# Rotary embedding of queries and keys: half-head rotation by four shifted copies on ScalarE in place of a TensorE product

## What is computed

```python
def apply_rope(t, cos, sin):
    half = t.shape[-1] // 2
    tf = t.astype(jnp.float32)
    t1, t2 = tf[..., :half], tf[..., half:]
    return jnp.concatenate([t1 * cos - t2 * sin, t2 * cos + t1 * sin], axis=-1).astype(t.dtype)
```

## Time and profile before

| | |
|---|---|
| median of 3 runs | 1289.53 us (1288.16 to 1290.08) |
| the profiled execution: its own time | 1289.31 us |
| the profiled execution: its span | 1287.7 us |
| PE busy | 1255.5 us, 98% of the span |
| DVE busy | 652.0 us, 51% |
| ACT busy | 270.4 us, 21% |
| granted TensorE clock, mean | 0.999 of full speed |

### The profile page before, as it was taken

The page is one execution under the profiler, slowest core; times in us unless marked ns, Lnnn a source line. Parts: engine busy times, 40 slices in busy tenths (PEclk is TensorE's granted clock), DMA queues, the critical chain, the costliest instruction groups (busy, mean ns, idle before and its releaser), DMA issues.

```text
span 1287.7 us, 26831 instructions
## 1 busy us (share of the span) xinstructions
PE 1255.5 (98%) x10748; PEld 953.2 (74%) x10748; DVE 652.0 (51%) x1636; ACT 270.4 (21%) x713; POOL 75.2 (6%) x134
## 2 busy tenths in 40 slices
PE   6999999999999999999999999999999999999997
PEld 4768888999999768689999997777764455445444
DVE  5355564888888533656677675664541011101104
ACT  4332304211111512630000013146300000000001
POOL 0100000000000000000000000100010000000020
PEclk9999999999999999999999999999999999999999
DMA  9999883577776672046776784894599999999990
GB/s 354 413 400 405 304 294 131 205 262 272 284 253 244 246 279 89 33 142 230 281 274 255 276 307 163 305 353 122 194 390 405 420 408 410 409 421 407 407 374 37
DMA packets 74181, 368.83 MB, mean 286 GB/s; under 512 B 8355, under 2 KB 8611, under 8 KB 49338
## 3 DMA queue, kind: packets, MB, share of 16 engines
q1 hardware_dynamic: 56594, 271.28, 55.5%
q0 software_dynamic: 17520, 96.64, 19.8%
HBM read 347.82 MB, written 20.06 MB: 286 GB/s over the span
## 4 chain that ended last, share of the span: by engine, by line
PE 94%; DVE 2%; ACT 2%; DMA 1%; SPq 1%; issue 0%; DVEq 0%
PE banks L972 20%; PE banks L704 18%; PE banks L1309 13%; PE banks L959 11%; PE banks L1358 9%; PE banks L1333 5%; PE banks L729 4%; PE banks L823 2%; PE banks L783 2%; PE banks L1039 2%; PE banks L888 1%; PE banks L872 1%; DMA ring<-stream 1%; PE banks L899 1%; PE banks L857 1%; PE banks L742 1%
## 5 line engine op out<-in xcount | busy, mean ns | idle before, releaser
L1750 DVE CUSTOM_DVE_ANT_0 side<-side 128x1024 f32<-128x1024 f32 x128 | 151.1, 1220 | 33.0 <-DMA side<-ada 32.9
L1309 PE MATMUL banks<-ring,arena 128*32 128x512 f32 x1536 | 166.3, 593 | 0.7 <-DVE arena L2232 0.7
L959 PE MATMUL banks<-arena,ring 128*128 128x256 f32 x704 | 160.2, 381 | 0.0
L704 PE MATMUL banks<-h,ring 128*128 128x256 f32 x640 | 143.5, 382 | 0.6 <-ACT arena L1408 0.3
L959 PEld LDWEIGHTS banks<-arena,ring 128*128 128x128 f32 x704 | 130.6, 191 | 16.8 <-issue 1.4
L704 PEld LDWEIGHTS banks<-h,ring 128*128 128x128 f32 x640 | 120.5, 190 | 21.7 <-issue 3.2
L1309 PEld LDWEIGHTS banks<-ring,arena 128*32 128x32 f32 x1536 | 50.1, 110 | 111.8 <-issue 110.8
L2335 DVE TENSOR_TENSOR arena<-arena,banks 128x256 f32<-128x256 f32 (+1 forms) x48 | 15.2, 330 | 178.5 <-ACT arena L1685 178.5
L704 PE MATMUL banks<-arena,ring 128*128 128x256 f32 x384 | 84.1, 380 | 0.5 <-ACT arena L1499 0.5
L972 PEld LDWEIGHTS banks<-h,ring 128*128 128x128 f32 x672 | 81.5, 192 | 2.0
L972 PE MATMUL banks<-arena 128*128 128x128 f32 x672 | 81.9, 276 | 0.0
(11 more groups left out here) (337 smaller groups left out, 1556.5 us busy)
## 6 DMA issues: line engine op xcount, KB each, us to landing
ring<-stream SPq DMA_DIRECT2D x247, 512.0 KB, 5.6
ring<-experts SPq DMA_DIRECT2D x96, 1024.0 KB, 14.8
side<-ada POOLq DMA_DIRECT2D x64, 1024.0 KB, 7.7
side<-experts SPq DMA_DIRECT2D x24, 1024.0 KB, 14.7
arena<-experts SPq DMA_DIRECT2D x8, 1024.0 KB, 14.8
yrows<-side POOLq DMA_DIRECT2D x1, 6144.0 KB, 42.4
hrows<-side POOLq DMA_DIRECT2D x1, 5632.0 KB, 20.4
arena<-lasts SPq DMA_DIRECT2D x8, 512.0 KB, 14.5
```

The costliest lines, as they stand in the source:

```text
L704: last = pe.matmul(bank(u, a, a + T), ring[:, s, (k0 + kc) * P:(k0 + kc + 1) * P], moving[:, kc, :], start=(kc == 0), stop=(kc == kn - 1))
L959: last = pe.matmul(banks[:, 4 + c // 2, (c % 2) * T:(c % 2 + 1) * T], ring[:, s, c * P:(c + 1) * P], hid[:, j % 2, :], start=False, stop=F ...
L1309: ins = pe.matmul(banks[BLOCK * j:BLOCK * (j + 1), t, :], hg[:, k, BLOCK * t:BLOCK * (t + 1)], ring[:, m, (j % 2) * 512:(j % 2 + 1) * 512] ...
L1750: dve.tensor_tensor_reduce(weights, weights, cond[:, 0 if layer0 else 1, :], 1.0, 0.0, ALU.mult, ALU.add, accum_out=msum[:, n:n + 1]).then ...
```

## The change

PE no longer rotates: the matrix `rotate`, the 20 rotation units and their places in the order of banks are gone. ACT makes the rotated tile instead, in `turn`: four copies of 32 partitions by 256, each from the neighbouring block of 32 partitions, with scale 1 or -1, into one of three buffers `ropet` in SBUF. The source is the PSUM bank, just before the bank is read by the usual copy (`take_turned`), or for r = 5 and 6 the tile in SBUF. From r = 3 on, ACT first waits until rope r-3 is complete. DVE multiplies the rotated tile by sin in place, in SBUF. With the rotation units gone, two projection units in a row are on different banks, where before a unit, a rotation and the next unit put the two units on the same bank.

```diff
-            def rotate(r, moving, ready):
-                u = U["rot", r]
-                begin(u)
-                pe.wait_ge(*ready)
-                pe.matmul(bank(u, 0, T), mat("rotate"), moving, start=True, stop=True).then_inc(aux_done, 1)
-
...
             between = {0: [lambda: one(("sq", 0))],
-                       1: [lambda: one(("sq", 1)), rot_of(0, "sq", 0, sqT[:, 0])],
-                       2: [lambda: one(("sq", 2)), rot_of(1, "sq", 1, sqT[:, 1])],
...
+                       1: [lambda: one(("sq", 1))],
+                       2: [lambda: one(("sq", 2))],
...
+            def turn(r, source):
+
+                if r >= 3:
+                    act.wait_ge(s_rope, r - 2)
+                for j in range(4):
+                    to, at = BLOCK * j, BLOCK * (j ^ 1)
+                    act.activation(ropet[to:to + BLOCK, r % 3, :], source[at:at + BLOCK, :], ACT.Copy, scale=(1.0 if j % 2 else -1.0))\
+                       .then_inc(s_turn, 1)
+
+            def take_turned(r, u, out):
+
+                act.wait_ge(*u.done)
+                turn(r, bank(u, 0, T))
+                take(u, out, 0, T)
...
-            take(U["iq", 1], iqT[:, 1, :], 0, T)
+            act.wait_ge(s_raw, raw_step(4, 5))
+            turn(5, ikT)
+            turn(6, iqT[:, 0, :])
+            take_turned(7, U["iq", 1], iqT[:, 1, :])
             take(U["iwT"], iws.rearrange("p a n -> p (a n)"), 0, 16, scale=float(8 ** -0.5 * 64 ** -0.5))
             for c in range(2, 4):
-                take(U["iq", c], iqT[:, c, :], 0, T)
+                take_turned(6 + c, U["iq", c], iqT[:, c, :])
             for c in range(2):
-                take(U["dk", c], dkT[:, c, :], 0, T)
+                take_turned(10 + c, U["dk", c], dkT[:, c, :])
...
-            attend(odd_heads, {2 * (c - 4): [lambda c=c: take(U["dq", c], dqT[:, c, :], 0, T)] for c in range(4, 8)})
+            attend(odd_heads, {2 * (c - 4): [lambda c=c: take_turned(12 + c, U["dq", c], dqT[:, c, :])] for c in range(4, 8)})
...
             def rope(r, tile, source):
-                u = U["rot", r]
-                dve.wait_ge(*u.done)
-                dve.tensor_tensor(ropet[:, r % 2, :], bank(u, 0, T), sin[:, :], ALU.mult).then_inc(freed[u.bank], 1)
+                part = ropet[:, r % 3, :]
+                dve.wait_ge(s_turn, 4 * (r + 1))
+                dve.tensor_tensor(part, part, sin[:, :], ALU.mult).then_inc(s_rot, 1)
                 dve.wait_ge(*((s_raw, raw_step(4, 5)) if U[source].bank > 1 else taken(U[source])))
                 dve.tensor_tensor(tile, tile, cos[:, :], ALU.mult).then_inc(s_rot, 1)
-                dve.wait_ge(s_rot, r + 1)
-                dve.wait_ge(*taken(u))
-                dve.tensor_tensor(tile, tile, ropet[:, r % 2, :], ALU.add).then_inc(s_rope, 1)
+                dve.wait_ge(s_rot, 2 * r + 2)
+                dve.tensor_tensor(tile, tile, part, ALU.add).then_inc(s_rope, 1)
```

More of the change, by code:

```diff
@@ L72 @@
 MATS = {}
-for _name, _n in (("ident", 128), ("heads", 128), ("rotate", 128), ("causal", TRI), ("band", TRI),
+for _name, _n in (("ident", 128), ("heads", 128), ("causal", TRI), ("band", TRI),
                   ("upto", T), ("iota", CAP), ("small", 64)):
@@ L170, in plan_units @@
         add(("sq", c), 1)
-        add(("rot", c - 1))
     add(("sk", 0), 1)
-    add(("rot", 3))
     add("sv", 1)
-    add(("rot", 4))
     add_out("eo")
@@ L181, in plan_units @@
     add(("iq", 1), 1)
-    add(("rot", 5))
     add("iwT")
     add(("iq", 2), 1)
-    add(("rot", 6))
     add(("iq", 3), 1)
-    add(("rot", 7))
     add(("dk", 0), 1)
-    add(("rot", 8))
     add(("dk", 1), 1)
-    add(("rot", 9))
-    add(("rot", 10))
     add("dv", 2)
-    add(("rot", 11))
     add(("dq", 0), 1)
@@ L197, in plan_units @@
         add(("dq", c), 1)
-        add(("rot", 11 + c))
         if c == 4:
             add("rrow")
-    add(("rot", 19))
     add_out("oo")
@@ L326, in program @@
         cum = region(27, [T], 72)
-        ropet = region(29, [2, T])
+        ropet = region(29, [3, T])
         oT2 = region(32, [8, T])
@@ L386, in program @@
         s_forget, s_cum = sem("s_forget"), sem("s_cum")
-        s_rot, s_rope = sem("s_rot"), sem("s_rope")
+        s_rot, s_rope, s_turn = sem("s_rot"), sem("s_rope"), sem("s_turn")
         s_iscore, s_relu, s_isum, s_topk, s_dmask = (sem(n) for n in ("s_iscore", "s_relu", "s_isum", "s_topk", "s_dmask"))
@@ L1145, in sv_unit @@
                 token_unit(u, 1, 1, P, P, do_begin=False)
-            def rot_of(r, name, c, tile):
-                return lambda: rotate(r, tile, taken(U[name, c]))
             between = {0: [lambda: one(("sq", 0))],
-                       1: [lambda: one(("sq", 1)), rot_of(0, "sq", 0, sqT[:, 0])],
-                       2: [lambda: one(("sq", 2)), rot_of(1, "sq", 1, sqT[:, 1])],
-                       3: [lambda: one(("sq", 3)), rot_of(2, "sq", 2, sqT[:, 2])],
-                       4: [lambda: one(("sk", 0)), rot_of(3, "sq", 3, sqT[:, 3])],
-                       5: [sv_unit, rot_of(4, "sk", 0, skT)]}
+                       1: [lambda: one(("sq", 1))],
+                       2: [lambda: one(("sq", 2))],
+                       3: [lambda: one(("sq", 3))],
+                       4: [lambda: one(("sk", 0))],
+                       5: [sv_unit]}
             for k in range(5):
@@ L1165, in _ @@
             one(("iq", 1))
-            rotate(5, ikT, (s_raw, raw_step(4, 5)))
             few_per_token("iw")
             one(("iq", 2))
-            rotate(6, iqT[:, 0], (s_raw, raw_step(4, 5)))
             one(("iq", 3))
-            rotate(7, iqT[:, 1], taken(U["iq", 1]))
             one(("dk", 0))
-            rotate(8, iqT[:, 2], taken(U["iq", 2]))
             one(("dk", 1))
-            rotate(9, iqT[:, 3], taken(U["iq", 3]))
             def index_scores(m):
@@ L1190, in _ @@
             index_scores(1)
-            rotate(10, dkT[:, 0], taken(U["dk", 0]))
             u = U["dv"]
@@ L1196, in _ @@
                     index_scores(2 + n)
-            rotate(11, dkT[:, 1], taken(U["dk", 1]))
             one(("dq", 0))
@@ L1203, in step @@
                         one(("dq", c))
-                    rotate(11 + c, dqT[:, c - 1], taken(U["dq", c - 1]))
                 return step
@@ L1632, in _ @@
             take(U["fv", 1], fv[:, 1, :])
-            between = {c: [lambda c=c: take(U["sq", c], sqT[:, c, :], 0, T)] for c in range(4)}
-            between[4] = [lambda: take(U["sk", 0], skT, 0, T)]
+            between = {c: [lambda c=c: take_turned(c, U["sq", c], sqT[:, c, :])] for c in range(4)}
+            between[4] = [lambda: take_turned(4, U["sk", 0], skT)]
             between[5] = [lambda: take(U["sv"], sv.rearrange("p a n -> p (a n)"), 0, T)]
@@ L1654, in _ @@
             for c in range(4):
-                take(U["dq", c], dqT[:, c, :], 0, T)
-            attend(odd_heads, {2 * (c - 4): [lambda c=c: take(U["dq", c], dqT[:, c, :], 0, T)] for c in range(4, 8)})
+                take_turned(12 + c, U["dq", c], dqT[:, c, :])
+            attend(odd_heads, {2 * (c - 4): [lambda c=c: take_turned(12 + c, U["dq", c], dqT[:, c, :])] for c in range(4, 8)})
             squares(5)
@@ L2423, in _constants @@
     k, m = p, np.arange(P)[None, :]
-    put("rotate", (k == m - 32) * (m % HD >= 32) * 1.0 - (k == m + 32) * (m % HD < 32) * 1.0)
     dist = np.concatenate([p - np.arange(HALF)[None, :], HALF + p - t], 1)
```

## The result

The changed kernel takes 1291.56 us, the median of 14 runs (1288.95 to 1295.31), against 1289.08 (1288.16 to 1290.56, 14 runs) for the kernel before: a ratio of 1.0019, interval 1.0011 to 1.0028. I had forecast 1284.1 with a range up to 1289.4. The measured median lies outside the range, on the slower side; it is 2.5 us or 0.2% above the kernel before, which is also about what a measurement here can tell.

A forecast was written before the change was run, and what follows sets the result against it. PE, busy for 98% of the span, was taken as the bound. Over the 20 rotations, 4.9 + 1.6 + 1.0 + 0.7 - 0.65 - 2.3 = 5.2 us less gave 1289.31 - 5.2 = 1284.1 us, range 1280.5 to 1289.4.

The forecast's parts named there:

- the price of a turn: On ACT, four copies of 32 partitions at 0.28 us each, 1.12 us in front of the usual copy.
- second transpose behind the first: Attention steps of rotations 2, 16, 17, 18: PE's start goes from 1.59 to 2.17 us, 2.3 us more in all.
- iq2 behind the end of iq1: Rotation 5: iq1 and iq2 now share a bank, so iq2 waits for iq1's copy; 0.65 us more.
- index scores 2 behind the end of dk1: Rotations 9 and 10: start 2.2 us after dk1 instead of 2.88, so 0.7 us less.
- dq5 behind the end of dq4: Rotation 15: shared bank, start 1.76 us after dq4's end against 1.81 before; no change.
- the rival of the dear copies: Turns at 0.40 us a copy: seven places hanging on ACT pay 0.48 more each, 3.4 together, 1287.5 us; chance 0.13.
- the granted clock is 1.00 in both windows: PE stays at the 2.4 GHz level, busy throughout; the change leaves the clock as it is.
- The banks alternate: Rotations 1, 3, 6, 7, 8, 12, 13 between projection units: 3.5 us a unit instead of 4.19, 4.9 us less.
- ACT's wait for rope r-3 and the choice of keys: Rope wait put at nothing, a few tenths in the range; DVE's key choice at nothing, 1.3 us in the range.
- the rival "given back in the experts": Weights' DMA sets the pace in the experts, so arriving 5 us earlier helps nothing: 1289.3 us; chance 0.08.
- the hidden case: ACT's share is hidden, turns being cheap: each rotation gives back 0.6, 12 us less, 1277 us; chance 0.07.
- The four attention steps would pay: Rotations 2, 16, 17, 18: PE waits about 1.2 us for L1484 where it was 0.67; 4 x 0.58 = 2.3 us more.

The follow-up runs named there:

- The kernel whose waits are filled: Changed kernel plus 16 unused 128x256 products on PE ahead of iq2, dq5 and second transposes, where PE waits for ACT; 1287.21 us, ratio 0.9978.
- the last kernel: Copies turned in SBUF behind the usual copy, but turns 0, 1, 2, 4 directly behind their copies and turn 19 a step later; 1280.59 us, ratio 0.9918.
- the one-block kernel: Changed kernel with all four copies reading and writing partitions 0 to 31, rotation left out; 1283.08 us, ratio 0.9942.
- the profile without the shift: Changed kernel with each of the four copies reading the block it writes, so halves don't change places; 1291.46 us, one run.
- The kernel with alternating banks alone: Kernel before, products kept on PE, rotations 5 to 14 moved to banks 4 and 6 so successive units alternate banks; 1286.60 us, ratio 0.9978.
- the two kernels that split the condition: Changed kernel, rotation left out: one writes partitions 0 to 31 and reads four blocks (1293.71 us), the other the reverse (1292.45 us).
- the one with the usual copy first: Changed kernel with the usual copy freeing the bank first and the turn reading the SBUF tile behind it, later in attention steps; 1287.40 us, ratio 0.9978.

## Why the prediction was wrong

**The step that failed first is the price of a turn.** "I take 0.28, since these are also Copy from PSUM to SBUF without a pointer." The copies of the earlier trace rows all begin at partition 0, and they overlap. The new copies begin at partitions 0, 32, 64 and 96 in turn, and don't: 0.40. The run with everything in one block shows both at once, 0.27 and 1283.1 us. So at that price the rest of the sum was right, or 2 us too cautious. Why the step failed: I compared operation, shape and memory, and not where in the partitions the instruction before had begun; "the shift of partitions is unseen" stood among the rival's reasons only.

The Trainium skill, page "VectorE: DVE Perf Modes", section "Two Vector instructions with no wait between them", states a rule of this kind for VectorE: an instruction is held until all earlier ones have finished if its input or output starts in another quadrant of 32 partitions than the last one's there. The section is about VectorE; the kernels with 1.57, 1.17, 1.58 and 1.56 us behave as if ScalarE had the same rule.
The Trainium skill's page "ScalarE: Activation LUTs", section "What ACT_TABLE_LOAD costs", has 399 ns for such a copy and an overlap of 93 for copies in a row. An estimate from it with the overlap left out is 0.40 a copy and 1.60 a turn, as measured; with it, as I had set it beside the rows, the estimate is 306 ns, and the measured spacing of overlapping copies is 0.27.

**The places were right, their sizes not.** Where I said that PE hangs on ACT, each place came out some half a microsecond longer, and 4 x 0.12 = 0.48 is the difference in a turn:

- second transpose behind the first, in step 1 of the third layer: 1.59 before, 2.17 forecast, 856.86 - 854.15 = 2.71 measured;
- iq2 behind the end of iq1: 1.75 forecast, 798.97 - 796.58 = 2.39. Of the 0.64 more, 0.16 are turns 5 and 6: at 0.44 a copy they fill ACT from 793.43 to 796.91, past iq1's end, and turn 7 starts 796.94 - 796.58 = 0.36 behind it and not 0.2;
- index scores 2 behind the end of dk1: 2.2 forecast, 817.16 - 814.55 = 2.61;
- dq5 behind the end of dq4: 1.76 forecast, 850.59 - 848.34 = 2.25. I had put this place at no cost.

That is the rival of the dear copies, 7 x 0.48 = 3.4 us, 1287.5. I gave it 0.13. The kernel whose waits are filled, in which this loss stands almost alone, took 1287.2. So the dear copies alone, as I had priced them, leave a gain; they don't turn the sign.

**The second failure is a sentence and not a number**: "the granted clock is 1.00 in both windows [...]; the change leaves it so." I added to PE's waits for ACT in the plan and priced them at their length. Behind them the granted clock fell to the 1.2 GHz level in the profiles. In the changed kernel's first one, from 501.69 on, sixteen records and a unit took 9.0 us (501.69 to 510.7), where the kernel with copies in one block needed 507.37 - 501.64 = 5.7: a wait of 2.22 us cost 3.3 more behind it. From iq2 on, 64 records took 15.65 instead of the 14.08 of the last kernel, another 1.6. No rival had this; together with the first failure it makes the sign. The filled waits put it at 4.3 us by the medians, at (1.0019 - 0.9978) x 1289.1 = 5.3 by the ratios. With the first, 1284.1 + 3.4 + 4.3 = 1291.8, against 1291.56 measured; the last term is an outcome and not a forecast, but both failures are needed to reach it. That it fits so closely is partly luck. By the ratios, on 1289.1, the one-block kernel stands at 1281.6, the filled one at 1286.2 and the changed one at 1291.5: the sum was 2.5 too cautious, the copies cost 4.6 and the clock 5.3.

The traces give the clock's part more directly. From the first transpose at 500 us to the first product of the experts (930.61 - 498.54 = 432.07 in the first profile) it is 424.01 us with filled waits and no low stretch, 428.75 without the shift and with two stretches, 432.07 and 432.30 in the two profiles of the changed kernel with four each. Two of the four (at 502 and 857 us) stand behind waits of 2.2 us in all five profiles with dear copies and unfilled waits; of the others one is behind iq2, and one has no long wait ahead.

**What held.**

- The banks alternate: 3.48 a unit in the third layer, against 4.19. The kernel with alternating banks alone shows that of the 0.7 some 0.3 is the bank and 0.4 the product.
- ACT's wait for rope r-3 and the choice of keys cost nothing to be seen: PE's scores start at 843.27 instead of 844.85 and, like those at 848.55, without a wait.
- The experts: 44.00 of 44.00 us at 412 GB/s, like the earlier trace rows. The gain of the one-block kernel reached the end undiminished, so the rival "given back in the experts" falls, and the hidden case too, since 1277 was never reached with turns ahead of the copies.
- The four attention steps would pay: yes, but with waits of 2.22 in two of them and 1.42 in the other two, not 1.2. The 1.2 was also too short for my own sum: the rotation's 0.43 of PE is gone from the gap of 2.17, and the one-block kernel has the 2.15 with a wait of 1.67.

**What stays open.** Which wait lowers the clock in which execution isn't settled. Behind iq2 the clock fell in both profiles of the changed kernel, after a wait of 2.11 us. In the profile without the shift the wait there is 1.98 and the window this:

```profile
798.00:802.00 4.00, 2.90 (x13) 2.58 (x14) 3.97 (x8) 1.07 (x4) 0.53 (x1) 1.00 0.28 70
```

There the clock stays at 1.00, and the 64 records take 14.08 us; so they do in the two kernels that split the condition, after waits of 2.28 and 1.97. The length of the wait alone doesn't decide it. From 504 to 508 it is 0.50 in all of these. That the two groups of the changed kernel's times are executions with fewer and with more such stretches is likely, from the clocks listed with them and from the 3.3 us between two stretches and four, but only two of its executions were profiled, and both belong to the upper group or above it.

## What to carry to other kernels

Take the price of a short ACT instruction from instructions that follow one another as the new ones will: same memory, and the same start partitions from one to the next; where they change, count full durations. On an engine that feeds a busy PE, put the copy that frees the bank or the scores first and work for later behind it, and then look who needs that later work; 80 copies of the same size gave 1291.6, 1287.4 or 1280.6 us by their place, the last two although their source in SBUF made each copy dearer. And a wait put into a PE-bound kernel costs its length plus what the clock may lose behind it.

## What the runs showed of the hardware

- **ACT's overlap depends on start partitions.** Copies of 32x256 come 0.27 us apart when each starts at the same partition as the one before (1.17 for four), 0.40 when either the read or the write side moves to another block (1.57, 1.58, 1.56). The single copy takes 362 ns in the former and 375 in the latter. From SBUF it is the same: eight in 2.75 us with one start, in 3.48 with changing ones.
- **A source in SBUF is dearer for ACT than one in PSUM**: 414 against 375 ns, for the same copy to SBUF.
- **The clock falls behind some short waits, and not only there.** Behind waits of 2.2 us it was at 0.50 to 0.60 in the windows at 504 and 856; in the changed kernel a unit takes 5.39 us from 914 on, with no wait ahead of it. PE's timeline:

```profile
911.56 2.74 PE L835 MATMUL banks<-vectors,h 128*128 128x8 f32 x24
...
914.16 5.39 PE L692 MATMUL banks<-arena,ring 128*128 128x256 f32 x16
```

  What stands ahead are 12 products of 8 columns each (24 records), for which PE counts as busy; the window behind it was at 0.68. The same unit takes 5.39 us in the profiles of the one-block kernel and of the one with the usual copy first, 5.21 in the last kernel's, and 3.70 in the other seven, the kernel before and the second profile of the changed kernel among them. What decides it isn't shown.
- **Useless work can pay.** 16 products (32 records) that nobody reads, in the waits, took 4.3 us off the median.
